# Seven block products instead of eight for four of eight row pairs in a feed-forward's second product

## What is computed

```python
D_MODEL, SEQ, D_FF = 2048, 256, 8192

def squared_relu_mlp(h, w1, w2):
    return jnp.square(jax.nn.relu(h @ w1)) @ w2

x = x + squared_relu_mlp(rms_norm(x, norm_ffn_g[l]), w_ff1[l], w_ff2[l])
return rms_norm(x, final_norm_g)
```

## Time and profile before

| | |
|---|---|
| time, median of 3 runs | 1606.21 us (1606.19 to 1606.55) |
| span of the profiled execution | 1604.8 us, 1.4 us under that median; no time of its own is given beside the span |
| TensorE busy | 1595.9 us of it (99%) |
| VectorE busy | 1252.5 us (78%) |
| ScalarE busy | 866.1 us (54%) |
| moved by DMA | 304.97 MB, 190 GB/s on the mean |

### The profile page before, as it was taken

The page is one execution under the profiler, slowest core; times in us unless marked ns, Lnnn a source line. Parts: engine busy times, 40 slices in busy tenths (PEclk is TensorE's granted clock), DMA queues, the critical chain, the costliest instruction groups (busy, mean ns, idle before and its releaser), DMA issues.

```text
span 1604.8 us, 22691 instructions
## 1 busy us (share of the span) xinstructions
PE 1595.9 (99%) x7962; PEld 1352.9 (84%) x7962; DVE 1252.5 (78%) x1681; ACT 866.1 (54%) x1120; POOL 75.9 (5%) x160
## 2 busy tenths in 40 slices
PE   9999999999999999999999999999999999999998
PEld 8888888888888888888888888888888888888886
DVE  5588889999989898786887665885677666866587
ACT  7444456555555556754566655454464455545555
POOL 6500010000000000000000000000000000000001
PEclk9999999999999999999999999999999999999999
DMA  7665645555555665556664566666666666666555
GB/s 256 203 192 184 196 151 171 177 176 174 184 171 170 210 207 181 200 183 238 210 197 138 164 186 191 201 198 190 190 211 196 182 185 196 197 197 187 192 187 182
DMA packets 161294, 304.97 MB, mean 190 GB/s; under 512 B 11689, under 2 KB 20513, under 8 KB 160801
## 3 DMA queue, kind: packets, MB, share of 16 engines
q1 hardware_dynamic: 160128, 300.45, 58.9%
q0 software_dynamic: 1056, 3.46, 0.6%
q10 hardware_dynamic: 32, 0.01, 0.0%
HBM read 301.78 MB, written 2.10 MB: 189 GB/s over the span
## 4 chain that ended last, share of the span: by engine, by line
PE 98%; DVE 1%; DMA 1%; issue 0%; ACT 0%; SPq 0%; ACTq 0%; POOL 0%; DVEq 0%; POOLq 0%
PE ps L2255 15%; PE ps L1750 12%; PE ps L1752 12%; PE ps L1751 12%; PE ps L2025 9%; PE ps L2024 9%; PE ps L2023 9%; PE ps L2257 7%; PE ps L1763 1%; PE ps L1929 1%; PE ps L2146 1%; PE ps L1932 1%; PE ps L1914 1%; PE ps L1913 1%; PE ps L1912 1%; DMA raw<-in_w_ff_dram 1%
## 5 line engine op out<-in xcount | busy, mean ns | idle before, releaser
L1079 DVE TENSOR_TENSOR w_both<-raw,w_both 128x1024 fp32r<-128x1024 f32 x538 | 656.6, 1223 | 257.0 <-ACT w_both L624 255.3
L624 ACT ACTIVATE w_both<-raw 128x1024 fp32r<-128x1024 f32 x538 | 568.7, 1060 | 527.7 <-PE ps L1752 181.7
L2255 PE MATMUL ps<-a_both,w_both 128*128 128x512 f32 x1024 | 321.9, 396 | 0.0
L1750 PE MATMUL ps<-w_both,a_both 128*128 128x512 f32 x636 | 252.4, 397 | 0.1
L1752 PE MATMUL ps<-w_both,a_both 128*128 128x512 f32 x636 | 248.3, 390 | 0.0
L1751 PE MATMUL ps<-w_both,a_both 128*128 128x512 f32 x636 | 248.2, 390 | 0.0
L2257 PEld LDWEIGHTS ps<-a_both,w_both 128*128 128x128 f32 x1024 | 192.5, 188 | 45.2
L1140 DVE SCALAR_TENSOR_TENSOR acc<-hconv,cwk,acc 128x256 f32<-128x256 f32 x464 | 205.1, 497 | 7.4 <-PE ps L1968 7.4
L2257 PE MATMUL ps<-a_both,w_both 128*128 128x256 f32 x1024 | 201.4, 278 | 0.0
L2023 PE MATMUL ps<-w_both,c_hi 128*128 128x512 f32 x504 | 196.7, 390 | 0.3 <-DVE w_both L1079 0.3
L2025 PE MATMUL ps<-w_both,c_lo 128*128 128x512 f32 x504 | 196.4, 390 | 0.0
(11 more groups left out here) (377 smaller groups left out, 1920.3 us busy)
## 6 DMA issues: line engine op xcount, KB each, us to landing
raw<-in_w_ff_dram SPq DMA_DIRECT2D x256, 512.0 KB, 4.1
raw<-in_w_in_dram SPq DMA_DIRECT2D x144, 512.0 KB, 3.6
raw<-in_w_mla_out_dram SPq DMA_DIRECT2D x32, 512.0 KB, 3.7
raw<-in_w_conv_out_dram SPq DMA_DIRECT2D x32, 512.0 KB, 4.3
raw<-in_w_out_dram SPq DMA_DIRECT2D x32, 512.0 KB, 4.5
raw<-in_w_ukv_dram SPq DMA_DIRECT2D x16, 512.0 KB, 3.8
raw<-in_w_xkv_dram SPq DMA_DIRECT2D x16, 512.0 KB, 4.0
raw<-in_w_uq_dram SPq DMA_DIRECT2D x16, 384.0 KB, 3.3
```

Of the source, the lines that this page charges most:

```text
L624: act.activation(whi[:, s, :], raw[:, s, :], ACT.Copy).then_inc(hi_ready, 1)
L1079: dve.tensor_tensor(wlo[:, s, :], raw[:, s, :], whi[:, s, :].bitcast(F32), ALU.subtract).then_inc(lo_ready, 1)
L1750: pe.matmul(sum_, x_hi[:, k0 + k, tok], w_hi, start=(first and k == 0), stop=False)
L2255: pe.matmul(both, whi[:, s, cols[n]], a_both[:, :, k0 + k, :], start=(first and k == 0), stop=False)
```

## The change

Four row pairs (m = 0 to 3) instead of two are done with seven products in each of the 8 passes. The weight blocks of a row pair are loaded a second time, as one transfer of 2 row tiles x 1024 columns (1 MB), into one of three slots (`t_raw`), and are summed in place there by VectorE (`t_sums`), copied to a high part by ScalarE (`t_high`) and lowered in place by VectorE in one operation of 2048 (`t_low`). Three of a group's eight blocks are prepared during the first product, the other five during the second. The second half of the right unit alone is loaded by the ring. The right unit now makes all five remaining products of its row pair, each kind into a bank of its own: M1, M5, M6 and M7 join the four output banks, so a pass uses all eight. After a pass VectorE sums M1, M5, M6, M7 (`m_sums`) into two tiles; it adds the first to `xres` itself (`add_m_sum`), and GpSimd issues a transfer that adds the second, except in the last pass, where VectorE adds it too (`add_m_neg`). The order of units, the waits between passes and groups, and the tail's conditions change with it; the loop over groups in SyncE's block is written out.

```diff
-LAST_LEFT, LAST_RIGHT = (3, 8), (4, 9)
+FF_ORDER = ((1, 8), (0, 8), (0, 0), (1, 0), (0, 10), (0, 2), (1, 2), (0, 12), (0, 4), (1, 4),
+            (1, 10), (0, 6), (1, 6), (0, 14), (1, 12), (1, 14))
+FF_LEFT, FF_RIGHT = (2, 5, 8, 11), (3, 6, 9, 12)
+LAST_ORDER = ((0, 8), (0, 10), (0, 0), (1, 0), (0, 12), (0, 2), (1, 2), (0, 14), (0, 4), (1, 4),
+              (0, 6), (1, 6), (1, 8), (1, 10), (1, 12), (1, 14))
+LAST_LEFT, LAST_RIGHT = (2, 5, 8, 10), (3, 6, 9, 11)
+SLOTS = 3
+M1_BANK, M7_BANK = 4, 5
+M6_BANK, M5_BANK = (6, 0), (7, 1)
+T_LOAD_FF1 = {(0, 5): 0, (1, 2): 1, (2, 2): 2}
+T_PREP_FF1 = {(0, 6): 0, (1, 4): 1, (3, 4): 2}
+T_LOAD = {(0, 10): 3, (0, 13): 4, (1, 0): 5, (1, 3): 6, (1, 10): 7}
+T_PREP = {(0, 8): 3, (0, 11): 4, (1, 1): 5, (1, 4): 6, (1, 8): 7}
...
+            def load_blocks(g, j):
+
+                p, m = j // FM, j % FM
+                src = w_ff2[:, ds(g * KT + 2 * m, 2), 2 * NC * p:2 * NC * (p + 1)]
+                if j < SLOTS:
+                    sp.wait_ge(chunk_out, g * CH + N_FF)
+                else:
+                    sp.wait_ge(m_done, g * FJ + (j - SLOTS + 1))
+                sp.dma_start(t_raw[j % SLOTS][:].rearrange("p (k c) n -> p k (c n)", k=2), src).then_inc(t_landed[j % SLOTS], 16)
...
+            for n in range(2 * GROUPS - 1):
+                c = 2 * (n % 2) + 1
+                pool.wait_ge(chunk_out, N_FF + 2 * n + 2)
+                pool.wait_ge(m_summed, 4 * (n + 1))
+                pool.dma_start(xres[:, :, NC * c:NC * (c + 1)], m_neg[:], accum_op=ALU.add).then_inc(neg_added, 16)
...
+            def t_high(g, j):
+
+                act.wait_ge(t_made, g * (3 * FJ) + 3 * (j + 1))
+                act.activation(t_hi[j % SLOTS][:], t_raw[j % SLOTS][:], ACT.Copy).then_inc(t_hi_ready, 1)
...
+            def t_sums(g, j):
+
+                t, done = t_raw[j % SLOTS], 3 * j
+                dve.wait_ge(t_landed[j % SLOTS], g * (16 * len(range(j % SLOTS, FJ, SLOTS))) + 16 * (j // SLOTS + 1))
+                dve.tensor_tensor(t[:, T1:T3 + 1, :], t[:, B11:B12 + 1, :], t[:, B12::2, :], ALU.add).then_inc(t_made, 1)
+                dve.wait_ge(t_made, g * (3 * FJ) + (done + 1))
+                dve.tensor_tensor(t[:, T2, :], t[:, B22, :], t[:, T1, :], ALU.add).then_inc(t_made, 1)
+                dve.wait_ge(t_made, g * (3 * FJ) + (done + 2))
+                dve.tensor_tensor(t[:, T4, :], t[:, B21, :], t[:, T2, :], ALU.add).then_inc(t_made, 1)
+
+            def t_low(g, j):
+
+                dve.wait_ge(t_hi_ready, g * FJ + (j + 1))
+                dve.tensor_tensor(t_lo[j % SLOTS][:], t_raw[j % SLOTS][:], t_hi[j % SLOTS][:].bitcast(F32), ALU.subtract).then_inc(t_lo_ready, 1)
+
+            def m_sums(g, p):
...
+                dve.tensor_tensor(m_sum[:, 1, :], ps[:, M6_BANK[p], :], m_sum[:, 0, :], ALU.add).then_inc(m_summed, 1)
...
+                dve.scalar_tensor_tensor(out=m_neg[:, 0, :], in0=m_sum[:, 1, :], scalar=-1.0, in1=ps[:, M5_BANK[p], :],
+                                         op0=ALU.mult, op1=ALU.subtract).then_inc(m_summed, 1)
+                dve.wait_ge(m_summed, done + 2)
+                dve.tensor_tensor(m_sum[:, 1, :], ps[:, M7_BANK, :], m_sum[:, 1, :], ALU.add).then_inc(m_summed, 1)
+                dve.tensor_tensor(m_neg[:, 1, :], m_neg[:, 0, :], ps[:, M7_BANK, :], ALU.subtract).then_inc(m_summed, 1)
...
                     for k in range(FF2_UNITS):
                         if p == 0 and k == 0:
                             ff_add(CH - 1, g * CH + CH)
                         i = k + LEAD
-                        if i in left:
-                            w_sums(g, p, left.index(i), U_FF + u, r, left)
+                        if (p, k) in T_PREP:
+                            t_sums(g, T_PREP[p, k])
+                        if (p, k - 1) in T_PREP:
+                            t_low(g, T_PREP[p, k - 1])
+                        if k == 15:
+                            dve.wait_ge(used, r + (U_FF + u + c0_done))
+                            if not first:
+                                dve.wait_ge(mixed, g * 2 + (MIXED_FF + p - 1))
+                            add_chunk(p, 0)
                         if i in right:
                             lo_second(U_FF + u + i, r)
...
-                        if k == right[1] + 2:
-                            dve.wait_ge(p4_done, g * 2 + (p + 4))
-                            add_chunk(p, 0)
-                        if k == right[1] + 3:
-                            add_copies(g, p, g * CH + (N_FF + 2 * p + 1))
-                            add_ones(g, p)
-                            add_last(g, p)
-                        if k == 13 and ends:
+                        if k == right[-1] + 2:
+                            m_sums(g, p)
+                        if k == 15:
+                            add_m_sum(g, p)
+                        if k == 15 and ends:
+                            add_m_neg()
                             gain(2)
...
+            def stream_pair(g, p, u, r, order, left, right, first_use):
...
+                    if i in left:
+                        m = left.index(i)
+                        mm = into(m1, hidden(2 * m, 0), slot(i, 0), i)
+                        if m == FM - 1:
+                            mm.then_inc(y_step, 1)
+                        into(banks[0], hidden(2 * m + 1, 0), slot(i, 1), i).then_inc(used, 1)
+                    elif i in right:
+                        m = right.index(i)
+                        pe.wait_ge(h_lo_ready, g * 2 + (m // 2 + 3))
+                        into(banks[1], combined(3, m), slot(i, 1), i).then_inc(used, 1)
+                        pe.wait_ge(t_lo_ready, g * FJ + (FM * p + m + 1))
+                        into(m6, combined(1, m), weight_sum(T2, m), i)
+                        into(banks[0] + 1, hidden(2 * m + 1, 1), weight_sum(T4, m), i)
+                        into(m5, combined(0, m), weight_sum(T1, m), i)
+                        into(m7, combined(2, m), weight_sum(T3, m), i).then_inc(m_done, 1)
```

More of the change, by code:

```diff
@@ L1026, in ff_group @@
                     ends = last and p == 1
-                    right, sums = (LAST_RIGHT, (1, 7)) if ends else (RIGHT, (5, 10))
+                    right = LAST_RIGHT if ends else FF_RIGHT
                     for k in range(FF2_UNITS):
                         n = UPC * CH + FF2_UNITS * p + k + LEAD
-                        if k == right[1]:
-                            y_out(g, p, 0)
                         if k + LEAD in right:
@@ new lines, in add_m_sum, with add_m_neg @@
+            def add_m_sum(g, p):
+                dve.wait_ge(m_summed, g * 8 + (4 * p + 3))
+                dve.wait_ge(chunk_out, g * CH + (N_FF + 2 * p + 1))
+                cols = xres[:, :, 2 * NC * p:2 * NC * p + NC]
+                dve.tensor_tensor(cols, m_sum[:], cols, ALU.add).then_inc(mixed, 1)
+            def add_m_neg():
+                dve.wait_ge(m_summed, 8 * GROUPS)
+                dve.wait_ge(neg_added, 16 * (2 * GROUPS - 2))
+                cols = xres[:, :, 3 * NC:]
+                dve.tensor_tensor(cols, m_neg[:], cols, ALU.add).then_inc(mixed, 1)
@@ L1673, in ff_group @@
                     ends = last and p == 1
-                    left, right, lows = (LAST_LEFT, LAST_RIGHT, ((1, 2), (7, 8))) if ends else (LEFT, RIGHT, ((5, 6), (10, 11)))
+                    order, right = (LAST_ORDER, LAST_RIGHT) if ends else (FF_ORDER, FF_RIGHT)
+                    c0_done = max(i for i, (c, _) in enumerate(order) if c == 0) + 1
                     u = UPC * CH + FF2_UNITS * p
@@ L1703, in ff_group @@
                         dve.wait_ge(used, r + (U_FF + u + FF2_UNITS))
[L1704 removed]
+                        if not first:
+                            dve.wait_ge(neg_added, g * 32 + (16 * p - 16))
                         add_chunk(p, 1)
@@ L2025, in product, with seven_pair @@
                 return pe.matmul(ps[:, bank, :], x_lo, w_hi, start=False, stop=last, skip_group_check=True)
-            def seven_pair(g, p, u, r, banks, first_use, between, sums, b=late, x_hi=c_hi, x_lo=c_lo, order=FF2_ORDER, left=LEFT, right=RIGHT):
+            def seven_pair(g, p, u, r, banks, first_use, between, sums, b=late, x_hi=c_hi, x_lo=c_lo):
                 def hidden(k, t):
```

236 lines of the change are left out of this document (179 added, 57 removed).

## The result

The changed kernel takes 1610.17 us (median of 9 runs), the kernel before 1606.23: ratio 1.0024, 95% interval 1.0014 to 1.0034. One of the nine runs of each was far slower (4132.39 us changed, 1761.92 before) and is left out of the ratio; the other eight of the changed kernel took 1609.65 to 1612.28. That is a little over 1609.4, from where the prediction called it slower, and 1.2 us over its forecast of 1609.0. The profiled execution spans 1607.8 us, 3.0 more than before (1604.8); 2.8 was forecast.

What follows compares the result with a forecast made beforehand. TensorE, 99% busy, was taken as the bound, VectorE as nearest second. Terms: -10.9 + 3 x 2.7 + (1.2 + 1.8) + 2.6 = +2.8 us, so the median 1606.2 becomes 1609.0; range 1599 to 1618.

Steps and rivals of the forecast that it cites:

- What goes: On TensorE, 48 matmuls fewer over 8 passes: 10.9 us off, 2.72 per group.
- What comes on VectorE: Per weight block 2.59 us of sums and 2.2 of low part; a second product's VectorE sum is 71.9 of 81.6 us.
- The waits of the second pass: TensorE waits for late VectorE splits and the next group's first matmul: 2.7 us in each of the first three groups.
- Boundary: The next group's first matmul waits 1.0 to 1.1 us for `add_chunk(1,0)`, which stands behind `m_sums`.
- The last group: In its second product, two waits as in the other groups (1.2 us) and 1.8 at right unit 11.
- The last right unit's sums: Right unit 11 of the last group: sums wanted at 28.5 of the pass, made at 30.3, so 1.8 us late.
- The tail: After the last pass, VectorE's sums beside GpSimd's multiplications make the second token half 2.6 us late, between 0 and 4.
- The first product: VectorE's 69.2 of 89.2 us are hidden; each unit behind a block is ready over 2 us early.
- A: The forecast: VectorE's rows eat the saving; 1605 to 1613 us, chance 0.42.
- C: Loads come late, with waits for DMA in every pass; slower, 1614 to 1621 us, chance 0.28.
- B: VectorE keeps up and second-pass waits vanish: 1601.2 us, or 1595.3 if boundaries and tail hide too; chance 0.30.

Runs made afterwards that it cites:

- e3: The changed kernel with the sums cut in two and, in the second product, a block's copy and low part one step later; 1603.03 us.
- e5: e3 with SyncE's first block loads of a group waiting for `m_done` instead of `chunk_out`; 1599.26 us.
- e1: The changed kernel with `m_sums` cut in two, its last two operations moved behind `add_chunk(p, 0)`; 1610.27 us.
- e2: The changed kernel with ScalarE's copy and VectorE's low part of a block one step later, in the second product alone; 1603.56 us.
- e9: e5 with `fin_g` and `fin` in memory the last first product leaves, `fin_g` fetched earlier, GpSimd's multiplications begun after VectorE's last split; 1597.76 us.
- e4: The changed kernel with GpSimd's transfers of `m_neg` moving 32 of 512 columns, the others left out of that sum; 1609.04 us.
- e7: e1 with SyncE's first block loads of a group waiting for `m_done` instead of `chunk_out`; 1605.00 us.

## Why the prediction came out as it did

**What goes: right.** 48 matmuls less, and where nothing waits (e3, e5) a group's second product is 2.74 us shorter, the whole of 2.72.

**What comes on VectorE: right in size.** The low part of a block is 2.21 from start to start (2.2 taken), the copy 1.92 (1.93), `m_sums` 2.64 (2.75), a second product's DMA rate 252 GB/s (244).

**The waits of the second pass: right, to 0.2 us.** Unit 5: 0.1 predicted, 0.05 + 0.11 in the first group and a second matmul 0.10 late, as behind a wait, in the others. Unit 8: 1.1, measured 0.98 + 0.11. Unit 12: 0.4, measured 0.23 + 0.11. Boundary: 1.0 to 1.1, measured 0.97, 0.91 and 0.91, each + 0.11. The restart was taken at 0 and is the 0.11. e1 and e2 show the cause, an order: each moves the operations that nobody waits for and takes away its own waits.

**The last group: right in the sum, wrong in a place.** Its first two waits were taken over from the other groups, 1.2 at units 5 and 8. Measured is 1.06 in front of the second pass's first matmul: the last order begins with a unit of c=0, whose banks wait for `add_chunk(0, 0)`, and TensorE, once late there, isn't early for the blocks. e1, with that sum earlier, has no wait there and 0.95 + 0.11 at the block instead. The last right unit's sums: 1.8 predicted, 1.67 + 0.11 measured.

**The tail: right in the sum (2.6, measured 2.4), not in its parts.** The slowing beside GpSimd was taken at 2 us; in the changed kernel it is 0.9, all in `add_m_sum`. One row behind the 2 us was misread: the add of the earlier trace rows that was said to go from 1.14 to 1.36 lasts its usual 1.23, and only the operation behind it starts later; it reads a PSUM bank, as do `m_sums` and `add_chunk`, which GpSimd didn't slow here. So the second token half starts 2.40 us behind the last matmul's start instead of 0.43, 2.0 more and not 2.6. The half itself, to the end of the span, takes 7.28 us where it took 6.88; in all kernels with the change it is 7.24 to 7.28. It now follows the first half 2.9 to 3.2 us later and not 4.0, which may be the reason; that was not tested. By the rule weighed there (the Trainium skill, SBUF — State Buffer, Who interferes with whom) `add_m_sum` would have waited out a GpSimd operation, 1.5 us by the prediction's estimate. The trace agrees with the rule, and the size was too high: `add_m_sum` waited out the rest of one operation, 0.9 us. What the same section of the Trainium skill says of an operation with at most one SBUF input, that GpSimd doesn't hold it up, is what e5 and e9 show, 0.68 us beside GpSimd as elsewhere.

**The first product: wrong, the step that failed.** "Hidden by TensorE's own work; followed step by step, each unit behind a block is ready over 2 us before TensorE wants it" left out SyncE's queue. It had weighed SyncE's wait for `m_done` in front of a block, but not the one for `chunk_out` in front of a first product's first block, nor the loads that stand behind that. The transfer of `m_neg` was taken as hidden if it lands in 35 us; it lands in 7.0 to 11.9, but beside those loads: with it narrowed, 1.2 of the 1.5 us go (e4), and with the queue freed nothing is lost either (e7, e5), so in the changed kernel it takes both to make the loads late enough to matter. The step costs 1.2 us in the changed kernel (the other 0.3 are the restarts behind the three boundaries), and 3.7 once the boundary is clear (e1). In the sum other terms covered it, and that is luck: the three second products took 1.0 less than forecast (0.6 of it a wait that one of them had in the kernel before), the tail 0.2 less. So the spans differ by 3.0, with 2.8 forecast; the medians differ by 3.9, and the interval of the ratio, 2.3 to 5.5 us, holds both.

**The rivals.** A, the forecast, is what happened. C, late loads in every pass, is refuted for the second passes by e4 and e5. Its sign is there in part: in the four second passes ScalarE waits 22.8 us in sum for loads, 9.9 before. But in e5 it waits 22.3 there, and TensorE is busy throughout the first three second products. The lateness that C named costs time elsewhere, in the first products. B, VectorE keeps up, is not what the changed kernel does, but what it can do: with the same work in another order (e5) it is 1599.3 us, under the 1601.2 that B had for the case that the second pass's waits vanish. The section that B draws on (the Trainium skill, Perfetto Trace Analysis, Identifying the Most-Contended Engine) judges TensorE by the arithmetic it achieves or by its weight loads, not by its matmul time; the weight loads are busy 84% in the earlier trace rows, still the highest, so its advice is the same here.

**What the change is worth.** e9, with the change and four edits of order and place, beats both kernels: 1597.76 us, 0.52% under the kernel before. Of the 10.9 us it loses 1.1 on TensorE in front of the last right unit and 1.4 in the tail; that leaves 8.4, and 8.3 is measured between the medians (9.2 between the profiled spans, 0.6 of it the wait that the kernel before had there in its third second product).

## What to carry to other kernels

When work moves from an engine that is 99% busy to one that is 78% busy, the mean says that it fits and the order decides: ask for each operation who waits for it and when, and put those that nobody waits for yet behind those that somebody does. Follow the queues of the transfer engines as far as those of the compute engines: one wait for an early load in front of others makes all of them late, and a short wait further up can hide it until it is mended. An edit that takes away a wait and gains nothing can have uncovered the next one, as e1 did; look at the stage lengths, not at the time alone.
